# A feed-forward layer in two passes: squared hidden values kept in DRAM, and the second matmul as seven half-size products summed in PSUM banks

## What is computed

```python
h = rmsnorm(x, g_ffn[i])                                   # 1024 x 1024
x = x + jnp.square(jax.nn.relu(h @ w_ff1[i])) @ w_ff2[i]   # w_ff1 1024 x 4096, w_ff2 4096 x 1024
gate = jax.nn.sigmoid(rmsnorm(x, g_ple[i]) @ w_ple_gate[i])
x = x + gate * (p[i] @ w_ple_proj[i])
```

## Time and profile before

| | us |
|---|---|
| median of 3 runs (1073.83 to 1074.12) | 1074.12 |
| span of the profiled execution, first to last instruction | 1072.1 |
| PE busy | 1063.0 (99%) |
| DVE busy | 680.3 (63%) |
| ScalarE (ACT) busy | 468.1 (44%) |
| POOL busy | 416.6 (39%) |
| moved by DMA | 61.06 MB, 57 GB/s in the mean |

### The profile page before, as it was taken

How to read it: one execution, slowest core, us unless ns; L and a number is a source line. 1 busy time by engine, 2 the same in 40 slices (tenths; PEclk the granted TensorE clock), 3 DMA queues, 4 the chain that set the end, 5 groups by cost and what they waited for, 6 DMA issues and landing times.

```text
span 1072.1 us, 13889 instructions
## 1 busy us (share of the span) xinstructions
PE 1063.0 (99%) x4960; PEld 869.5 (81%) x4960; DVE 680.3 (63%) x932; ACT 468.1 (44%) x806; POOL 416.6 (39%) x282
## 2 busy tenths in 40 slices
PE   9999999999999999999999999999999999999997
PEld 7877787777887888888888888888888888888897
DVE  7988787888799643644544544544544544697648
ACT  7467836555683332332332322322322422566334
POOL 0000061334136626516426425435435445295221
PEclk9999999999999999999999999999999999999999
DMA  8111110111011121121111111112112112420004
GB/s 335 40 40 40 40 58 32 40 41 40 0 40 40 40 79 39 39 78 39 39 70 48 39 49 69 39 39 78 39 39 78 39 39 76 159 79 1 1 2 158
DMA packets 20179, 61.06 MB, mean 57 GB/s; under 512 B 2096, under 2 KB 4144, under 8 KB 20144
## 3 DMA queue, kind: packets, MB, share of 16 engines
q1 hardware_dynamic: 19312, 59.56, 15.3%
q10 hardware_dynamic: 832, 1.05, 0.3%
HBM read 56.40 MB, written 4.19 MB: 57 GB/s over the span
## 4 chain that ended last, share of the span: by engine, by line
PE 89%; DVE 6%; ACT 3%; issue 1%; DMA 1%; SPq 0%; POOL 0%; DVEq 0%; ACTq 0%; POOLq 0%
PE bank L611 29%; PE bank L612 28%; PE bank L613 28%; PE bank L726 1%; PE bank L697 1%; ACT raw L1191 1%; DMA stage<-in_w_in 1%; DVE xT L1849 1%; DVE t_lo L1798 1%; PE bank L741 0%; PE bank L756 0%; DVE raw L1792 0%; ACT h_hi L1183 0%; DVE r_ffn L1433 0%; DVE r_mix L1433 0%
## 5 line engine op out<-in xcount | busy, mean ns | idle before, releaser
L611 PE MATMUL bank<-h_hi,w_hi 128*128 128x512 f32 (+1 forms) x722 | 278.5, 386 | 0.6 <-DVE w_lo L1428 0.5
L612 PE MATMUL bank<-h_lo,w_hi 128*128 128x512 f32 (+1 forms) x722 | 274.6, 380 | 0.0
L613 PE MATMUL bank<-h_hi,w_lo 128*128 128x512 f32 (+1 forms) x722 | 274.5, 380 | 0.0
L1849 DVE TENSOR_TENSOR xT<-bank,xT 128x512 f32<-128x512 f32 x256 | 172.3, 688 | 109.8 <-PE bank L613 109.8
L611 PE MATMUL bank<-u_hi,w_hi 128*128 128x512 f32 x512 | 199.8, 390 | 0.2
L613 PE MATMUL bank<-u_hi,w_lo 128*128 128x512 f32 x512 | 199.2, 389 | 0.0
L612 PE MATMUL bank<-u_lo,w_hi 128*128 128x512 f32 x512 | 199.2, 389 | 0.0
L611 PEld LDWEIGHTS bank<-h_hi,w_hi 128*128 128x128 f32 x722 | 135.7, 188 | 35.1 <-issue 6.6
L613 PEld LDWEIGHTS bank<-h_hi,w_lo 128*128 128x128 f32 x722 | 135.8, 188 | 26.1
L612 PEld LDWEIGHTS bank<-h_lo,w_hi 128*128 128x128 f32 x722 | 135.8, 188 | 25.4 <-issue 0.5
L557 POOL TENSOR_TENSOR w_lo<-w_raw,w_hi 128x1024 fp32r<-128x1024 f32 x30 | 73.9, 2485 | 125.6 <-ACT w_hi L1283 117.8
(11 more groups left out here) (238 smaller groups left out, 1727.9 us busy)
## 6 DMA issues: line engine op xcount, KB each, us to landing
w_raw<-in_w_ff SPq DMA_DIRECT2D x60, 512.0 KB, 3.8
stage<-in_w_in SPq DMA_DIRECT2D x13, 512.0 KB, 6.6
stage<-in_w_out SPq DMA_DIRECT2D x8, 512.0 KB, 4.5
stage<-in_w_ple_gate SPq DMA_DIRECT2D x8, 512.0 KB, 3.2
xT<-in_x SPq DMA_DIRECT2D x6, 512.0 KB, 10.9
stage<-in_w_ff SPq DMA_DIRECT2D x4, 512.0 KB, 3.2
out_x<-xT SPq DMA_DIRECT2D x4, 512.0 KB, 3.1
out_x<-xT SPq DMA_DIRECT2D x6, 256.0 KB, 2.2
```

The source lines that it names most:

```text
L611: pe.matmul(o, whi, hh, start=first, stop=False, skip_group_check=onto)
L612: pe.matmul(o, whi, hl, start=False, stop=False, skip_group_check=onto)
L613: return pe.matmul(o, wlo, hh, start=False, stop=last, skip_group_check=onto)
L1849: dve.tensor_tensor(dst, bank[4 + q % 4][:, :], dst, ALU.add).then_inc(y_added, 1)
```

## The change

The feed-forward becomes two passes.

**Pass 1** computes the hidden values of all 16 blocks. Blocks 0 and 1 are made plainly (2 x 96 matmuls), blocks 2 to 15 by the seven products (84 each, loop L1043 from block 3). There is no `ff2` between them: each block ends in its squared quarters and four sums of them (`sum_t1` to `sum_t4`), which SP writes to DRAM arrays `u_b22`, `u_t12`, `u_b21` (512 KB a block each) and `u_b11` (256 KB). DVE also makes the sums of w_ff2's quarters for one block at a time (`w2_pair`, 4 additions), and SP writes them to `w2_sums` (1 MB a block). The factor `r_ffn` is read from banks 4 and 5 and some squares from banks 6 and 7.

**Pass 2** is the second matmul over all 4096 hidden features, as seven half-size products of 16 steps: 112 steps, written out one by one. A step has 4 output tiles of 128 and 512 tokens, one tile deep: 12 matmuls. A product is summed over its 16 steps in four banks (0 to 3 or 4 to 7, in turn), and only then does DVE add it to the one to four quadrants of `xT` that it belongs to (`QUADRANTS`; 52 additions in all, two per step from step 4 of the next product on). For each step SP loads a left operand (w_ff2 or a sum) and a right operand (hidden values or a sum), 256 KB each; ScalarE makes both high parts, POOL the left low part, DVE the right low part. They lie in a ring of eight slots, and of four in the last product, where the other four slots' place holds gate weights:

```diff
-            def ff2(b):
-                for hf in range(2):
-                    pe.wait_ge(u_ready, 4 * b + (2 * hf + 2 + RING_FREE))
-                    for m in range(KD):
...
-                        pe.wait_ge(y_added, 16 * b + (q + 1))
-                        for k in range(2):
...
-                            last = passes(o, w_hi[:, n2, c:c + P], w_lo[:, n2, c:c + P], hh, hl, k == 0, k == 1)
-                        last.then_inc(ff2_done, 1)
+            for s in range(STEPS):
+                i, n = s // FF_BLOCKS, s % FF_BLOCKS
+                o = ring_slot(s)
+                pe.wait_ge(left_ready, s + 1)
+                pe.wait_ge(right_ready, s + 1)
...
+                if n == 0 and i >= 2:
+                    pe.wait_ge(y_added, ADDS_BY[i - 2])
+                for m in range(LT):
...
+                    last = passes(bank[4 * (i % 2) + SUM_BANKS[m]][:, :], left_hi[o][:, m * P:(m + 1) * P],
+                                  left_lo[o][:, m * P:(m + 1) * P], right_hi[o][:, :], right_lo[o][:, :], n == 0,
+                                  n == FF_BLOCKS - 1)
+                last.then_inc(step_done, 1)
+                if s == 107:
+                    pe.wait_ge(y_added, ADDS_BY[5])
+                    sum_rows(SS_PLE, acc2, 7)
```

SP's load of a step, and the ring:

```diff
+        def ring_slot(s):
+            return s % 8 if s < NARROW else 4 + s % 4
+        def ring_before(s):
+            return s - 8 if s < NARROW else s - 4
+            def load_step(s):
+                i, n = s // FF_BLOCKS, s % FF_BLOCKS
+                o, g, e = ring_slot(s), n // 2, n % 2
+                if s >= 8:
+                    step_over(sp, ring_before(s))
...
+                sp.dma_start(left_raw[o][:, :], src).then_inc(ring_in[o], 16)
...
+                sp.dma_start(right_raw[o][:, :], src).then_inc(ring_in[o], 16)
```

`NARROW` is 96. `w2_sums` of blocks 13 to 15 are made in steps 13 to 18 of pass 2 and written at steps 22 to 27. POOL's and DVE's lists in pass 2:

```diff
+            for s in range(STEPS):
+                o = ring_slot(s)
+                pool.wait_ge(left_high, s + 1)
+                pool.tensor_tensor(left_lo[o][:, :], left_raw[o][:, :], left_hi[o][:, :], ALU.subtract
+                                   ).then_inc(left_ready, 1)
+                if 76 <= s < 84 and s % 2 == 0:
+                    add_square(pool, SS_PLE, (s - 76) // 2, sq3, acc2)
+                if 92 <= s < 100 and s % 2 == 0:
+                    add_square(pool, SS_PLE, LT + (s - 92) // 2, sq3, acc2)
+                if s == 100:
+                    total_rest(pool, SS_PLE)
+                if s in (102, 104):
+                    low(2 * GATE_FIRST + (s == 104))
+                if 106 <= s < 110:
+                    add_square(pool, SS_PLE + 1, s - 106, sq3, acc2)
...
+            for s in range(3, STEPS):
+                right_low(s)
+                i, n = s // FF_BLOCKS - 1, s % FF_BLOCKS - 4
+                if i >= 0 and 0 <= n < ADDS[i] // 2:
+                    product_add(i, 2 * n)
+                    product_add(i, 2 * n + 1)
...
+                if 105 <= s < 109:
+                    ple_low(s - 105, 1)
+                if s in (109, 110):
+                    w_low(2 * GATE_FIRST + 2 + s - 109)
+            for j in range(LT):
+                product_add(PRODUCTS - 1, j)
```

More of the change, by code:

```diff
@@ L85 @@
 PRODUCTS = 7
+PLAIN = 2
+STEPS = PRODUCTS * FF_BLOCKS
+NARROW = STEPS - FF_BLOCKS
+SUM_BANKS = (0, 1, 3, 2)
+QUADRANTS = (((LT, 0), (0, 0), (LT, 1), (0, 1)), ((LT, 0), (0, 0), (LT, 1)), ((LT, 0), (0, 0)), ((LT, 0), (LT, 1)),
+             ((0, 0),), ((LT, 1),), ((0, 1),))
+ADDS = [LT * len(q) for q in QUADRANTS]
+ADDS_BY = [sum(ADDS[:i + 1]) for i in range(PRODUCTS)]
+LATE_SETS = (13, 14, 15)
+FF_ORDER = tuple(range(LT, KD)) + tuple(range(LT))
 WARM, WARM_END = 9, 7
@@ L468, in _ @@
+            for i in range(2, GATE_PIECES):
+                load_piece(GATE_FIRST + i, w_ple_gate, i)
             out_tiles = out.rearrange("(k p) t -> p k t", p=P)
@@ L581, in _ @@
+            for i in range(LT, KD):
+                add_square(pool, SS_PLE + 1, i, sq3, acc2)
             total_rest(pool, SS_PLE + 1)
@@ new lines, in _ @@
+            t_high_part(1)
+            square_b11((0, 0, 1))
+            act.wait_ge(ff1_done, 4)
+            act.wait_ge(w_split, 2 * (FF_FIRST + 2))
+            w1_high_part((2, 0, 1), 0, 32, 0)
+            square_b21((0, 0, 1))
+            t_high_part(2)
+            for i in range(1, 5):
+                w1_high_part((2, 0, 1), 0, 32, i)
+            t_high_part(4)
+            first_part(1)
+            for hf in range(2):
+                act.activation(bank[4 + hf][:, :], r_ffn[:, half(hf)], ACT.Copy).then_inc(r_banked, 1)
@@ new lines, in _ @@
+            t_high_part(3)
+            act.wait_ge(t_ready[3], LT)
+            for i in range(5, PRODUCTS):
+                w1_high_part((2, 0, 1), 0, 32, i)
+            square_b11((1, 0, 1))
+            square_b21((1, 0, 1))
+            with act.Fori(0, 6) as g:
+                ff_block((2, g, 2), 1, 32 * g + 32)
+                ff_block((3, g, 2), 0, 32 * g + 64)
+            ff_block((14, 0, 1), 1, 32 * 7)
+            first_bank((15, 0, 1))
+            step_high(0)
+            step_high(1)
@@ L1878, in _ @@
+            sum_t3((0, 0, 1))
+            for k in range(LT):
+                t_make(1, k)
+            first_relu(0, 2)
+            first_relu(0, 3)
+            for k in range(LT):
+                t_make(2, k)
+            sum_t1((0, 0, 1))
+            sum_t2((0, 0, 1))
+            for k in range(LT):
+                t_make(4, k)
+            sum_t4((0, 0, 1))
+            for i in (1, 2):
                 for k in range(LT):
                     t_low(i, k)
-            with dve.Fori(1, FF_BLOCKS - 1) as b:
-                hidden(b)
-                for q in range(16):
-                    add_ff(b, q)
@@ L1899, in _ @@
-            for i in range(6):
-                split_low(H_PLE + KD + i, xT[:, i, half(1)], v_ple[:, i:i + 1], i, 1)
+            first_relu(1, 1)
+            first_relu(1, 0)
+            for k in range(LT):
+                t_low(4, k)
+            sum_t3((1, 0, 1))
+            for k in range(LT):
+                t_low(3, k)
+            first_relu(1, 2)
+            first_relu(1, 3)
+            sum_t1((1, 0, 1))
+            sum_t2((1, 0, 1))
+            sum_t4((1, 0, 1))
+            dve.wait_ge(r_banked, 2)
@@ L1901, in _ @@
+            for j in range(LT):
+                product_add(PRODUCTS - 1, j)
+            for i in range(LT, 6):
+                ple_low(i, 1)
             invert(SS_PLE, r_mix)
```

802 lines of the change are left out of this document (481 added, 321 removed).

## The result

| | before | changed | ratio |
|---|---|---|---|
| median of 4 runs each, us | 1074.12 | 1046.32 (1045.69 to 1047.63) | 0.974, 95% interval 0.9726 to 0.9754 |
| span of the profiled execution, us | 1072.1 | 1044.7 | |

A forecast was written before the change was run, and what follows sets the result against it. PE was taken to bound the kernel, busy 1063.0 of 1072.1 us. The span 1072.1 - 40.8 (180 matmuls) + 3.0 (last product) = 1034.3, with 2.0 around it, gave 1036.3 us; range 1032.5 to 1047.

The forecast's parts named there:

- a loss in the last product alone: Forecast case: only the last product of pass 2 loses, 1 to 6 us; time 1034.3 to 1039.3 us, chance 0.56.
- prediction's own signs of being wrong: PE waiting on bank 0 or 3 reads in pass 1, waits spread over pass 2, or matmul distance not 0.227 us.
- Matmuls removed, -40.8 us: Feed-forward: first matmul +12, second -192, net 180 fewer at 0.2269 us each, the whole gain.
- Pass 1 inside a block, 0: Pass 1 blocks: DVE, ACT and POOL work all fits into PE's 19.06 us a block; cost 0.
- The two reads with 2 us of room: Pass 1: DVE's reads of banks 0 and 3 come 2.0 us before PE needs those banks; cost 0.
- DMA in pass 1, 0: Pass 1: 4.98 million bytes a block, 261 GB/s, against 330 to 385 when full; cost 0.
- The price of the sums of w_ff2: Pass 1: DVE's four `w2_pair` operations a block at 0.69 us each, within its 11.7 us of work.
- The last product, +3: Pass 2, steps 96 to 111: POOL 2.1 us late from excess work, ACT's third and fourth square adding; +3 us.
- Start of pass 1, 0: Between block 0's first matmul and the first product: PE has 192 matmuls as before, DVE loses 16 additions; cost 0.
- Steps 13 to 18, "12 us of room, which swallows `w2_pair`": Pass 2: eight slots let loads start seven steps ahead, leaving 12 us of room for late w_ff2 sums; cost 0.
- Transition to pass 2, 0: From pass 1 to 2: step 0's operands come during block 15, step 3's right operand 4 us before it is due; cost 0.
- The rival of many small stalls: Pass 1: each of 14 blocks loses about 0.7 us at tight bank reads behind stores; 10 us, 1046, chance 0.18.

The follow-up runs named there:

- run 10: Changed kernel, with each of the ten blocks of SP's pass 1 loop also copying 1 MB of w_ff1 to an unused DRAM array: 1043.48 us.
- run 9: Changed kernel, with `right_low(2)` in block 15 moved behind DVE's reads of bank 2: 1048.37 us.
- run 2: Changed kernel, with POOL starting block 2's w_ff1 sums only after DVE's first eight `t_low`: 1047.98 us.
- run 1: Changed kernel, with DVE's reads of banks 1 and 2 (`first_relu`, block 1) put ahead of the eight `t_low`: 1046.25 us.
- run 3: Changed kernel; POOL waits for eight `t_low`, DVE makes `t_low(4)` behind `t_low(1)` and `t_low(2)`, ACT makes t4's and t3's high parts before w_ff1's: 1040.01 us.
- run 4: Changed kernel, with DVE making `t_low(4)` earlier and ACT t4's and t3's high parts first, but POOL not made to wait: 1041.98 us.

## Why the prediction was right, and where it wasn't

It named the sign, the measured time lies in its range (at its upper end), and its main term held. But the likeliest case, a loss in the last product alone, didn't come: the losses were 13.6 us net in place of 3.0. That the time lies in the range is luck in part, since the range reached to 1047 only for a rival whose mechanism didn't come; the forecast case ended at 1039.3. One of the prediction's own signs of being wrong came, waits of PE in pass 2 outside the last product (B and C).

- *Matmuls removed, -40.8 us*: right. 180 fewer, the distance unchanged; products that change bank every three matmuls run at the same 0.2267.
- *Pass 1 inside a block, 0*: right but for the loop edges, which I had counted as nothing and which took 0.1 each, six times. The two reads with 2 us of room never stopped PE. *DMA in pass 1, 0*: right, 254 GB/s measured (261 worked out), and room above it (run 10). The price of the sums of w_ff2 was too low, 0.69 us each on DVE: they took 1.07 to 1.63 in the mean, hidden all the same.
- *The last product, +3*: right in place and size (3.7), and in the cause as far as POOL's excess of work and ACT's third and fourth square, which waited for POOL by 2.75 and 1.97 us. But the sum let POOL's left operand be the late one, and the sign was to be waits of PE on `left_lo`. All four of PE's waits there ended with DVE's `right_lo` instead, 2.3 us in all. DVE's own list in these steps had no sum.
- *Start of pass 1, 0*: the step that failed most. I wrote that DVE loses 16 additions there. True, but those additions read a bank and don't conflict with POOL; they had stood between the t_low operations. Without them the t_low come one after another, each beside a POOL operation, at 1.64 us; and I didn't see that the reads which free banks 1 and 2 are queued behind them. It cost 5.9 where the kernel before lost 2.0 (0.9, 0.8 and 0.3), and 1.7 of it came by the lower clock, of which my sum had no term. The trace before already had a sign of it that I passed over. Between 330 and 334 us three weight loads wait for DVE, 1.70 us apart where six matmuls take 1.36: DVE, slowed by POOL, set PE's pace.

```profile
PEld bank L611 <- DVE xT L1849: 1.4, 3, 0.5
```

- *Steps 13 to 18, "12 us of room, which swallows `w2_pair`"*: failed. The queue was full, at 385 GB/s from 620 to 645 us, by the ring's first fill and 3 MB of late loads, so the lead was thin when the sums began, and two sums and a right operand took 5.1 us a step, where my price of 1.17 gives 3.5. It cost 3.8; thinned out, 1.1.
- *Transition to pass 2, 0*: 1.0. The right operands of steps 0 and 1 stand before DVE's read of bank 0, and beside POOL they took 2.53 us in place of 1.28 (run 9).

The common fault is in the price. From the earlier trace rows I took that DVE's operation on two SBUF operands rises to 1.17 us beside POOL. In that stretch each was followed by an addition from a bank. The period was 1.70 for one of each, and it is 1.64 to 1.70 too when there is no addition between: beside a row of POOL's, DVE finishes one such operation per POOL operation. So where POOL was first, DVE's price is the POOL operation's 1.29 and 0.41 of its own. Where DVE's row was first, DVE pays nothing and POOL pays the row: 3.58 and 3.48 us in place of 1.29.

The Trainium skill (SBUF — State Buffer, "SBUF: two separate sides") calls the shared port pair an exclusive lock on which the loser blocks. The trace agrees in kind: DVE's operation takes 0.61 us with POOL idle and 1.64 beside it (run 2), and in the timelines of runs 1, 3, 4 and the changed kernel the engine that was slowed had begun second. I had set the rule aside on POOL's side only, where DVE costs 0.41 and not its 0.68, and had overlooked what it says about DVE's side.

The rival of many small stalls gave 1046, which is what came, but by another mechanism: all but 0.1 us at some loop edges is lost at four places, and next to nothing inside the 14 blocks.

## What to carry to other kernels

Where a kernel is full of matmuls, the steady state is easily costed and the edges are where a rebuilt stage pays: check for each edge what stands in front of the operation that frees a bank or fills a slot. An engine operation's price depends on its neighbour engine: operations on two SBUF operands, issued in a row on DVE beside a POOL that was busy first, cost nearly three times their own duration (1.64 against 0.61 us here), and ones that read a bank cost nothing extra, so spread the former among the latter. When a stall is mended by order alone, look whether it only moves; here hold, order, spreading and moving the gate weights together took back 10.4 of 13 us.

## What I had not expected of the hardware

- DVE's 128x512 subtraction of two SBUF operands: 0.61 us each with POOL idle, 1.64 to 1.70 with POOL in a row of its own 1.29 us operations. In a row that DVE began first it stays at 0.61, and POOL's one operation takes 3.48 to 3.58.
- A wait of 2.04 us was followed by about 3 us of the lower clock (granted 0.68 over 5 us), when PE had been full for long before, apart from a few shorter waits. The next trace can differ: at C, where PE's starts lay 2.2 us further apart than usual, the clock fell in three runs (the changed kernel, 2 and 4) and stayed in run 1; at A it stayed behind 2.3 us in run 4 and fell behind 4.2 us each time. Behind the shorter ones, up to 2.0 us at C in run 3, it stayed in every run.
- The one queue moved 398 GB/s of 256 and 512 KB loads for 20 us (620 to 640 us), and 302 GB/s of mixed loads, stores and DRAM copies without PE losing anything.
